# Carrying an RMS norm's factor past the projections: squares and splits inside the output phases, the factor in the rotation tables, value and gate

## The reference, cut to what matters

```python
x = x + gate[:, None] * (mixed @ w_out)            # "out1"
x = rmsnorm(x, final_g)                            # "n1"
# second block, layer 0
h = rmsnorm(x, norm_ab) @ w_in_ab                  # "n2", then 8 "dil" heads and 4 "diff" heads
ya = dilated_mixture(rope(aq), rope(ak), av)
yb = diff_attention(rope(bq), rope(bk), bv, lam); yb = rmsnorm(yb, subln) * (1 - lam_init)
x = x + (concat(ya, yb) * silu(z)) @ w_out_ab      # "out2"
# layer 1
h = rmsnorm(x, norm_c) @ w_in_c                    # "n3", then 16 "caus" heads
x = x + (attention(rope(cq), rope(ck), cv) * silu(z)) @ w_out_c   # "out3"
return rmsnorm(x, final_norm)                      # "n4"
# rmsnorm(x, g) = x / sqrt(mean(x*x) + 1e-6) * g, the mean over the 2048 features of a token
```

## Time and profile before

| | us |
|---|---|
| median of 3 runs | 2777.7 (2775.08 to 2782.13) |
| the profiled execution | 2774.61 |
| its span | 2772.8 |
| TensorE matmul busy | 2554.3 (92%) |
| mean of a matmul of L182, L183, L184 | 0.296, 0.291, 0.291 |
| GpSimd busy | 1383.9 (50%) |
| VectorE busy | 1190.0 (43%) |
| ScalarE busy | 1182.5 (43%) |

### The profile page before, as it was taken

How to read it: one execution, slowest core, us unless ns; L and a number is a source line. 1 busy time by engine, 2 the same in 40 slices (tenths; PEclk the granted TensorE clock), 3 DMA queues, 4 the chain that set the end, 5 groups by cost and what they waited for, 6 DMA issues and landing times.

```text
span 2772.8 us, 65207 instructions
## 1 busy us (share of the span) xinstructions
PE 2554.3 (92%) x26246; PEld 2251.4 (81%) x26246; DVE 1190.0 (43%) x2009; ACT 1182.5 (43%) x1743; POOL 1383.9 (50%) x602
## 2 busy tenths in 40 slices
PE   6698999999999799988999989998899989999998
PEld 2276777777777688778999978998899979999997
DVE  5837676667667233333444114323222043332311
ACT  6642343334334233333444345444444355544443
POOL 0031221121222044336888857776677867777684
PEclk9998999999999799998999999999999999999999
DMA  8831111111111022217766533444444534444453
GB/s 308 272 112 48 59 42 44 49 63 42 43 58 48 19 88 87 83 61 263 239 237 238 188 121 110 163 160 145 138 153 161 183 101 165 149 161 159 159 179 117
DMA packets 97979, 361.32 MB, mean 130 GB/s; under 512 B 10880, under 2 KB 12032, under 8 KB 97440
## 3 DMA queue, kind: packets, MB, share of 16 engines
q1 hardware_dynamic: 96624, 354.95, 37.8%
q10 hardware_dynamic: 1200, 4.04, 0.4%
HBM read 356.85 MB, written 2.10 MB: 129 GB/s over the span
## 4 chain that ended last, share of the span: by engine, by line
PE 78%; issue 6%; DVE 5%; POOL 4%; ACT 4%; DMA 2%; SPq 0%; ACTq 0%; POOLq 0%; DVEq 0%
PE ps L182 16%; PE ps L184 15%; PE ps L183 15%; PE ps L574 5%; POOL wlo L170 4%; PE ps L575 3%; PE ps L576 3%; PE ps L660 2%; PE ps L724 2%; ACT whi L160 2%; DMA raw<-stream 2%; PE ps L745 1%; PE ps L1819 1%; PE ps L645 1%; PE ps L794 1%
## 5 line engine op out<-in xcount | busy, mean ns | idle before, releaser
L170 POOL TENSOR_TENSOR wlo<-raw,whi 128x1024 fp32r<-128x1024 f32 x563 | 1355.6, 2425 | 1318.5 <-ACT whi L160 1289.6
L182 PE MATMUL ps<-ahi,whi 128*128 128x256 f32 (+1 forms) x3712 | 1099.1, 296 | 62.4 <-POOL wlo L170 41.5
L183 PE MATMUL ps<-alo,whi 128*128 128x256 f32 (+1 forms) x3712 | 1079.3, 291 | 0.0
L184 PE MATMUL ps<-ahi,wlo 128*128 128x256 f32 (+1 forms) x3712 | 1078.7, 291 | 0.0
L182 PEld LDWEIGHTS ps<-ahi,whi 128*128 128x128 f32 x3712 | 719.2, 194 | 90.6 <-POOL wlo L170 50.0
L160 ACT ACTIVATE whi<-raw 128x1024 fp32r<-128x1024 f32 x566 | 585.8, 1054 | 355.4 <-PE ps L184 243.9
L183 PEld LDWEIGHTS ps<-alo,whi 128*128 128x128 f32 x3712 | 720.0, 194 | 8.7
L184 PEld LDWEIGHTS ps<-ahi,wlo 128*128 128x128 f32 x3712 | 719.4, 194 | 8.0
L574 PE MATMUL ps<-ahi,whi 128*128 128x256 f32 (+1 forms) x512 | 208.3, 407 | 2.9 <-ACT W L924 2.9
L575 PE MATMUL ps<-alo,whi 128*128 128x256 f32 (+1 forms) x512 | 176.0, 344 | 0.0
L576 PE MATMUL ps<-ahi,wlo 128*128 128x256 f32 (+1 forms) x512 | 175.7, 343 | 0.0
(11 more groups left out here) (321 smaller groups left out, 3276.6 us busy)
## 6 DMA issues: line engine op xcount, KB each, us to landing
raw<-stream SPq DMA_DIRECT2D x630, 512.0 KB, 3.3
graw<-stream SPq DMA_DIRECT2D x32, 512.0 KB, 5.3
W<-xT SPq DMA_DIRECT2D x1, 4096.0 KB, 18.1
XR<-xT ACTq DMA_DIRECT2D x1, 2048.0 KB, 8.3
outT<-XR SPq DMA_DIRECT2D x4, 512.0 KB, 2.6
cns<-consts SPq DMA_DIRECT2D x1, 1120.0 KB, 6.0
cns<-consts ACTq DMA_DIRECT2D x1, 896.0 KB, 11.4
W<-pair_par ACTq DMA_DIRECT2D x6, 146.0 KB, 2.2
```

Source lines behind the costliest of these rows:

```text
L170: nc.gpsimd.tensor_tensor(wlo[slot], raw[slot], whi[slot].bitcast(F32), ALU.subtract).then_inc(lo_done, 1)
L182: nc.tensor.matmul(out, whi[slot][:, k, :], mh, start=first and k == 0, stop=False)
L183: nc.tensor.matmul(out, whi[slot][:, k, :], ml, start=False, stop=False)
L184: ins = nc.tensor.matmul(out, wlo[slot][:, k, :], mh, start=False, stop=last and k == UK - 1)
```

## The change

- `norm_phase` is gone. In an out phase, as soon as tile g of `XR` is final, ScalarE writes the high part of x times gain (`ahi`, L1791) and the square (L1794; in out1 a second one, of x times `final_g`, L1796), VectorE the low part (`alo`), and adds the squares into PSUM bank 7. The gain of out1 is `final_g * norm_ab`.
- At the end VectorE copies the sums to SBUF (`accs`), one matmul by `meanw` adds over the partitions (L1890 of the new file), and root and reciprocal give `sr`. The head phases multiply by it where the projection's results are read: `sn` and `cs` are the rotation tables times the factor; v and gate tiles are multiplied by VectorE on their way out of PSUM.
- The first unit of the next phase is issued ahead of that matmul, the second behind it. For n1 and n2 both sums come from one pass (the second scale is the first plus a term in epsilon); the residual gets its n1 factor two tiles per dil head (`residual`).
- In every head loop TensorE does the next head's first unit ahead of O and its second behind O (in diff: between O and the sum for its norm). The first head's two units stand ahead of the loop, and diff's first two units come straight after the last dil head.
- `lam` is computed before out1 and at the end of out1.
- The order of the splits on ScalarE is changed: each head loop begins three units later (`hi(3)` first), and v's eviction is no longer ScalarE's.

The core of the diff (numbers, waits and semaphore names of the rest left out):

```diff
         def out_phase(...):
             def act_(act):
+                def tile(i, n):
+                    g = i * 2 + n
+                    x = XR[:, g, :]
+                    done.wait(act, g + 1)
+                    if gain is not None:
+                        nc.scalar.activation(ahi[:, 0, g, :], x, ACT.Identity, scale=gain[:, g:g + 1]).then_inc(N["hhi"].sem, 1)
+                    if g:
+                        N["acc"].wait(act, g)
+                    ins = nc.scalar.activation(sqv[:, n, 0:T], x, ACT.Square)
+                    if width > T:
+                        nc.scalar.activation(sqv[:, n, T:], x, ACT.Square, scale=pv[:, PV["final_g"]][:, g:g + 1])\
...
+                for i in range(KT // 2):
+                    tile(i, 0)
+                    for k in (3, 4): hi(i, k)
+                    tile(i, 1)
+                    for k in (5, 6): hi(i, k)
             def dve_(dve):
...
+                        if gain is not None:
+                            done.wait(dve, i * 2 + n + 1)
+                            N["hhi"].wait(dve, i * 2 + n + 1)
+                            nc.vector.scalar_tensor_tensor(alo[:, 0, gsl, :]..., x, gain[:, gsl], ahi[:, 0, gsl, :]..., ALU.mult, ALU.subtract)
+                        nc.vector.tensor_tensor(ps[:, 7, 0:width], sqv[:, n, 0:width], ps[:, 7, 0:width], ALU.add)
+                nc.vector.tensor_copy(accs[:, 0:width], ps[:, 7, 0:width]).then_inc(N["accs"].sem, 1)
-        def norm_phase(name, before, gain, split, count):
...
+        def dve_scales(dve, name, width):
+            N["mm"].wait(dve, 1)
+            nc.vector.tensor_scalar(sr[:, 0:T], ps[:, 7, 0:T], EPS, None, ALU.add)
+            if width > T:
+                nc.vector.scalar_tensor_tensor(sr[:, T:], sr[:, 0:T], EPS, ps[:, 7, T:], ALU.mult, ALU.add)
+            N["root"].wait(dve, 1)
+            nc.vector.reciprocal(sr[:, 0:width], sr[:, 0:width]).then_inc(N["r"].sem, 1)
+        def dve_tables(dve, name, s):
+            for new, old in ((sn, sin), (cs, cos)):
+                nc.vector.tensor_tensor(new, old, s2, ALU.mult).then_inc(N["tab"].sem, 1)
         def head_phase(...):
             def pe_(pe):
+                def body(i, more):
...
+                    if more:
+                        A["t1"].wait(pe, i + 1)
+                        unit(i, U_HEAD, ps[:, 0, 0:T], 0)
                     A["vt_ok"].wait(pe, i + 1)
                     A["pt_ok"].wait(pe, i + 1)
                     nc.tensor.matmul(ps[:, 6, 0:T], vt[:, 0, :], pt[:, 0:T], start=True, stop=False)
                     nc.tensor.matmul(ps[:, 6, P:T], vt[:, 1, :], pt[:, T:], start=False, stop=True)
+                    if more:
+                        unit(i, U_HEAD + 1, ps[:, 0, 0:T], UK)
             def act_(act):
-                    hi(0, 1, 2)
+                    hi(3)
                     for h in range(2):
                         nc.scalar.activation(rot[64 * h:64 * h + 64, :], ps[64 - 64 * h:128 - 64 * h, 0, :], ACT.Copy)
-                    hi(3)
-                    nc.scalar.activation(vf, ps[:, 1, 0:T], ACT.Copy)
-                    hi(4)
+                    hi(4, 5, 6)
                     for k in range(2):
                         A["nm"].wait(act, 2 * i + k + 1)
...
-                    hi(5)
-                    nc.scalar.activation(zz, ps[:, 2, 0:T], ACT.Tanh, scale=0.5)
+                    hi(7)
                     nc.scalar.activation(vt.rearrange("p c f -> p (c f)"), ps[:, 5, 0:T], ACT.Copy)
                     nc.scalar.activation(pt, ps[:, 4, 0:3 * P], ACT.Copy)
-                    hi(6, 7)
+                    A["zs"].wait(act, i + 1)
+                    nc.scalar.activation(ztan, zz, ACT.Tanh, scale=0.5)
+                    hi(8)
                     nc.scalar.activation(ahi[:, 1, bass.ds(i + y0, 1), :], yv, ACT.Copy)
+                    hi(9, 10)
             def dve_(dve):
+                    nc.vector.tensor_tensor(vf, ps[:, 1, 0:T], scale, ALU.mult)
...
+                    if residual:
+                        for r in range(2): nc.vector.scalar_tensor_tensor(x, x, final_g, sr[:, 0:T], ALU.mult, ALU.mult)
+                    nc.vector.tensor_tensor(zz, ps[:, 2, 0:T], scale, ALU.mult)
-                    nc.vector.scalar_tensor_tensor(zz, zz, 1.0, ps[:, 2, 0:T], ALU.add, ALU.mult)
+                    nc.vector.scalar_tensor_tensor(zz, ztan, 1.0, zz, ALU.add, ALU.mult)
```

More of the change, by code:

```diff
@@ new lines, in build, with pe_sums, act_root @@
+        accs = darea(512)
+        sr = darea(512)
+        cs = darea(512)
+        sn = darea(512)
+        def pe_sums(pe, name, width):
+            N = S[name]
+            N["accs"].wait(pe, 1)
+            nc.tensor.matmul(ps[:, 7, 0:width], meanw, accs[:, 0:width], start=True, stop=True).then_inc(N["mm"].sem, 1)
+        def act_root(act, name, width):
+            N = S[name]
+            N["a2" if width > T else "a1"].wait(act, 1)
+            nc.scalar.activation(sr[:, 0:width], sr[:, 0:width], ACT.Sqrt).then_inc(N["root"].sem, 1)
@@ new lines, in act_before_out1, with pe_after_out1, act_after_out1 @@
+        def act_before_out1(act):
+            L["gab"].wait(act, 1)
+        def pe_after_out1(pe):
+            pe_sums(pe, "out1", 2 * T)
+            L["m"].wait(pe, 2)
+            nc.tensor.matmul(ps[:, 6, 0:2], meanw, lamv[:, 0:2], start=True, stop=True).then_inc(L["lmm"].sem, 1)
+        def act_after_out1(act):
+            act_root(act, "out1", 2 * T)
+            L["lmm"].wait(act, 1)
+            nc.scalar.activation(lamv[:, 2:4], ps[:, 6, 0:2], ACT.Exp, scale=float(KT * P)).then_inc(L["lex"].sem, 1)
@@ L1907, in pe_ @@
                         .then_inc(A["o_mm"].sem, 1)
+                    if more:
+                        unit(i, U_HEAD + 1, ps[:, 0, 0:T], UK)
+                S[out]["done"].wait(pe, KT - 1)
+                for u in range(2):
+                    mm_unit(pe, (base + u) % RING, base + u, ps[:, 0, 0:T], 0, UK * u, u == 0, u == 1,
+                            tile_ready=lambda k: ready[0].wait(pe, k + 1))
+                    if u == 0:
+                        pe_between(pe)
+                with pe.Fori(0, heads - 1) as i:
+                    body(i, True)
+                body(heads - 1, False)
             def act_(act):
@@ L2045, in pe_ @@
                     ins.then_inc(B["o_mm"].sem, 1)
+                    if more:
+                        B["t1"].wait(pe, 2 * i + 2)
+                        unit(i, U_DIFF, ps[:, 0, 0:T], 0)
                     B["sq"].wait(pe, i + 1)
@@ L2049, in pe_ @@
                     ins.then_inc(B["ms_mm"].sem, 1)
+                    if more:
+                        unit(i, U_DIFF + 1, ps[:, 0, 0:T], UK)
+                for u in range(2):
+                    unit(0, u, ps[:, 0, 0:T], UK * u)
+                with pe.Fori(0, heads - 1) as i:
+                    body(i, True)
+                body(heads - 1, False)
             def act_(act):
-                B["lmm"].wait(act, 1)
-                nc.scalar.activation(lamv[:, 2:4], ps[:, 6, 0:2], ACT.Exp, scale=float(KT * P)).then_inc(B["lex"].sem, 1)
                 with act.Fori(0, heads) as i:
```

324 lines of the change are left out of this document (175 added, 149 removed).

## The result

The changed kernel takes 2669.9 us (median of 4 runs, 2663.7 to 2675.8), the kernel before 2779.9 us in the same comparison (4 runs, 2775.1 to 2782.6). The ratio is 0.9606 with a 95% interval of 0.9579 to 0.9632: some 110 us less.

The account below looks back on a forecast made before the run. TensorE, busy 92% of the span, bounds the kernel; 25.1 + 13.7 + 5.6 + 13.0 + 7.8 + 16.4 + 5.5 = 87.1 us take the profiled 2774.6 to 2687.5. Median 2691 us, own range 2675 to 2704, stated 2675 to 2724.

Parts of the forecast that it names:

- First seam: Out1 to dil, last `XR` addition to first QK: 31.5 us against 56.6, 25.1 us saved (20 to 34).
- Heads: Inside dil and caus heads: TensorE's waits for the gate tile's second unit and ahead of O go, saving 5.6 and 13.0 us.
- sum of 87.1: All terms of the forecast saving together, in us, from out1's last addition to the end.
- dil to diff: Between dil and diff: the 5.2 us wait for `lam`, its matmul and half the low clock go, 7.8 us saved.
- Diff: Diff heads and the last head's way into out2's first tile: 16.4 us saved together (12 to 19).
- 14.4 us: Diff's waits of TensorE without the last head's part, 15.0 less 0.6 for float32 to float32r changes; no clock counted.
- Second seam: Out2 to caus, last addition to first QK: 37.7 us before, QK at 21.6 plus 2.5 for clock, 13.7 saved (10 to 18).
- End: Last addition to the final norm's first operation (L1838): 8.21 us becomes 2.7, 5.5 us saved.
- Rivals 1 and 4: Heads gain nothing as splits come late, 2724 us (chance 0.12); the seams don't get shorter, 2730 us (chance 0.03).
- Rivals 2 and 3: Rotation one step more behind a split, 2747 us (0.08); behind two splits with clock falling in each head, 2817 us (0.04).
- rival 2: One rotation step more behind a split, QK late by up to 2.0 us in 28 heads: 2747 us, chance 0.08.

Follow-up runs that it names:

- late split: Changed kernel, but in dil and caus heads the split of the gate tile's second unit waits for v's end, behind a result-unused copy; 2720.9 us (0.9814).
- rotation through PSUM: Changed kernel, but no rotation step reads two SBUF operands: turned q and k and the cosine product stay in PSUM; 2659.8 us (0.9568).
- squares first: Changed kernel, but in out1 and out2 VectorE adds a tile's squares ahead of its low part, the last low part behind the sums' copy; 2661.1 us (0.9584).
- units behind O: Changed kernel, but both first units of the next head stand behind O again (in diff behind the matmul over the squares); 2687.2 us (0.9681).

## Why the prediction was right and wrong

**First seam (25.1, measured 25.7): right, by its steps.** The low part behind GpSimd, a gap of 2.7 (2.65), the root behind unit 5's split, tables and rotation behind one split after the other, a stall of 5.8 (6.6 from start to start), QK 31.5 us behind the addition (30.2), of which 4.5 were for the clock. That `lam` too would cost a full split (L1950, 2.19) was allowed for. The clock behind the stall ran on into the first head (26.61 instead of 24.95), which I had booked at the seam.

**Heads (5.6 and 13.0, measured 17.0 less 7.8 and 24.6): the term that was mis-sized, and the failed step.** The mechanism is the one forecast. The step that failed is the price of the two waits in a head of dil and caus: 0.8 us per caus head forecast, 1.6 measured. The size came from a view that can't give it: I took the waits (0.68 + 0.36 per caus head) and subtracted 0.2 for one more change from float32 to float32r. By distances of starts a caus head had 26.55 us and has 24.95. One of them before, from the gate tile's first matmul to the next head's first:

```profile
2598.17 0.47 PE L182 MATMUL ps<-ahi,whi 128*128 128x256 f32 x1
...
2601.76 0.39 PE L182 MATMUL ps<-ahi,whi 128*128 128x256 f32 x1 [0.36 <-POOL wlo L170]
...
2604.73 0.38 PE L1897 MATMUL ps<-cns,V 128*128 128x128 f32 x2
...
2606.12 0.67 PE L1905 MATMUL ps<-V 128*128 128x256 f32 x2 [0.68 <-ACT V L1934]
...
2606.85 0.36 PE L182 MATMUL ps<-ahi,whi 128*128 128x256 f32 x1
```

Gate tile: 6.56 us from QK to the transposes, 5.94 now (2508.58 to 2514.52), 0.62 for a wait shown as 0.36. Transposes and O: 2.12 us here (2.06 to 2.12 over the fifteen heads), 1.03 now, 1.09 for a wait shown as 0.68. The 0.2 for the change came to 0.09 (units 17.34, now 2.95 + 14.48). The wait column begins at the modelled end of the matmul before, where a next matmul would have started 0.25 us sooner; O itself, from its start to the next unit's, went from 0.73 to 0.57 us besides. The prediction had the better number at hand: its own sum of a head without waits, 25.4, is 1.1 below the 26.5 that a head took. Fifteen distances at 1.6 are 23.9 of caus's 24.6; in dil it was 7 x 1.5, less the 1.66 for the clock. That explains 11.6 + 3.6 of the 20.3 us by which the sum of 87.1 fell short.

**dil to diff (7.8): right.** The way from the last mask of dil to the first of diff is 8.2 us shorter (45.5 to 37.3).

**Diff (16.4, measured 16.9): right in sum by luck, wrong in its parts.** The 14.4 us come to 4.4 for each of the first three heads and 1.3 for the last. The three lost 5.3, 5.7 and 5.8 us, for the same reason as above and because the low clock behind the 2.3 us waits of three of the four heads, which I had not counted, went too (the 240 matmuls ahead of a head's QK took 29.94 to 30.38 us before, 29.77 with the new wait in them now). Against it stood two things that I had missed or taken too small: QK waits 0.55 for the rotation in three heads, and the last head ends in a stall of 3.8 us with the low clock behind it, where I had booked a gain of 3.3 with its gate tile; it gained 0.1.

**Second seam (13.7, measured 17.8): too cautious by two bounds.** I gave 2.5 us to the clock; it stayed at 1.00 behind the 2.1 us gap. And I put the second table behind a split and the rotation behind two, with QK 2.0 us behind the tiles; the tables fell into a pause of GpSimd (1.29 us together), and QK waited 0.2.

**End (5.5): right.** From the last addition to the first norm operation 2.73 us (forecast 2.7).

**The rivals.** Rivals 1 and 4 fell with the table above. Rivals 2 and 3, the rotation behind one or two more splits in every head, did not come in dil and caus: it still ends in time (QK waits 0.2 us once in caus). In diff the mild form of rival 2 did come, 0.55 us in three heads. The late split shows that the mechanism was not far: with four splits in a row at another place it cost 1.6 us per head.

**The range's** lower end (2675) was made of bounds for the seams and diff alone. The heads' terms, 18.6 of 87.1 us, had none, though their price came from a column whose zero is modelled. With the distances as the other end (24.6 instead of 13.0 for caus, 10.5 instead of 5.6 for dil) it would have reached down to 2675 - 11.6 - 4.9 = 2658.

## What to carry to other kernels

Price a wait that a change removes by the distance between the starts of the instructions around it, less the spacing they have when nothing waits; the idle column gives only a part where matmuls overlap. When a change gives VectorE operations on two SBUF operands (or fast copies and scalings in SBUF), look at where GpSimd runs back to back and where it pauses: the same two operations cost 1.3 us or 4.9. And when run times scatter in a part that the edit doesn't touch, compare from a common instruction on: here it told a loss of 1.7 us from a median that was 5 us better.

## What the runs showed of the hardware

VectorE waits for GpSimd not only with two SBUF operands. In the late split, L2086, a scaling of 128x128 and one of 128x256 in SBUF with one tensor operand, took 4.38 us for the two beside four GpSimd splits, 1.30 where one split ran beside the first and 0.55 where none did. A reduction of SBUF data (L2077, 0.61 for two, the second inside the same run) and a reciprocal of two columns (L2083, 0.17, inside it) took their plain times. The Trainium skill (SBUF — State Buffer, "Who interferes with whom") says this: besides operations with two SBUF inputs, copies and `tensor_scalar` may take the pair of ports that is shared with GpSimd, and `tensor_reduce` does not. The trace agrees. What has two operands and has to run beside a busy GpSimd should by the trace read one of them from PSUM, as the rotation through PSUM did; for copies and scalings no run here tries it.

An operation of one column waits as long as a large one: L1950 (128x1, two SBUF operands) took 2.19 us beside GpSimd's run and 0.16 in the pause.

The clock: behind the gap of 2.65 us at the first seam it was at 0.50, behind the 2.12 us at the second and the 1.12 us with the squares first at 1.00. Length alone doesn't decide: before the change TensorE waited 2.32 us at the same place in each of the four diff heads, and the granted clock was 1.00 behind the first (1949.7 to 1953) and 0.50 behind the second (2006.1 to 2008), and low behind the other two. Nor does the clock fall at the same point: behind the gap of 2.65 the two matmuls over the sums are 1.02 us apart in the changed kernel and 0.53 with the units behind O, where the low stretch began just behind them. That is worth 1.5 us at the seam. What decides it these runs don't show.
